# Chunk loop of a hybrid mLSTM decoder kernel: value weighting moved from GpSimd to ScalarE, mask addition moved from GpSimd to VectorE

## The reference

```python
a = g[..., None] - b + logi
m_new = jnp.maximum(g_j + m, a_j.max(-1))
w = jnp.exp(a_j - m_new[..., None])
C_new = decay[..., None, None] * C + jnp.einsum('bhl,bhld,bhle->bhde', w, k_j, v_j)
n_new = decay[..., None] * n + jnp.einsum('bhl,bhld->bhd', w, k_j)
...
log_d = jnp.where(causal, b[..., :, None] - b[..., None, :] + logi[..., None, :], -jnp.inf)
m_row = jnp.maximum(log_inter, log_d.max(-1))
p = jnp.einsum('bhcld,bhcsd->bhcls', q_c, k_c) * jnp.exp(log_d - m_row[..., None])
num = jnp.einsum('bhcls,bhcsd->bhcld', p, v_c) + w_inter[..., None] * jnp.einsum('bhcld,bhcde->bhcle', q_c, C_prev)
```

## Time and profile before

| | |
|---|---|
| median of 3 runs | 963.71 us (960.85 to 966.08) |
| the profiled execution, its own time | 963.89 us |
| its span, first to last instruction | 961.9 us |
| mean granted TensorE clock | 0.968 |
| TensorE products busy | 902.2 us (94%) |
| VectorE busy | 634.5 us (66%) |
| ScalarE busy | 454.6 us (47%) |
| GpSimd busy | 229.6 us (24%) |

### The profile page before, as it was taken

The page is one execution under the profiler, slowest core; times in us unless marked ns, Lnnn a source line. Parts: engine busy times, 40 slices in busy tenths (PEclk is TensorE's granted clock), DMA queues, the critical chain, the costliest instruction groups (busy, mean ns, idle before and its releaser), DMA issues.

```text
span 961.9 us, 15372 instructions
## 1 busy us (share of the span) xinstructions
PE 902.2 (94%) x5093; PEld 784.6 (82%) x5093; DVE 634.5 (66%) x945; ACT 454.6 (47%) x609; POOL 229.6 (24%) x239
## 2 busy tenths in 40 slices
PE   8999999999998899999889999999999999999930
PEld 8998887888776788888678988988988988988930
DVE  3432599895339877777874389385789974335727
ACT  4532101010258434422516489485789966345626
POOL 3100010001121121000022453453445442424410
PEclk9999999999999899999999999999999999999975
DMA  8620213111754444445486789888799997738256
GB/s 294 215 95 3 99 44 131 56 45 44 252 167 141 156 152 170 170 154 197 139 325 178 238 298 386 277 303 330 241 365 391 383 381 261 227 76 295 45 128 265
DMA packets 72963, 195.18 MB, mean 203 GB/s; under 512 B 9582, under 2 KB 23488, under 8 KB 72928
## 3 DMA queue, kind: packets, MB, share of 16 engines
q1 hardware_dynamic: 60976, 156.43, 44.5%
q0 software_dynamic: 11808, 38.15, 14.6%
q10 hardware_dynamic: 144, 0.14, 0.1%
HBM read 158.95 MB, written 35.74 MB: 202 GB/s over the span
## 4 chain that ended last, share of the span: by engine, by line
PE 89%; DVE 6%; issue 2%; DMA 1%; ACT 1%; POOL 0%; SPq 0%; DVEq 0%; POOLq 0%; ACTq 0%
PE banks L655 14%; PE banks L1155 14%; PE banks L644 14%; PE banks L669 14%; PE banks L1152 9%; PE banks L1295 9%; PE banks L1219 4%; PE banks L628 2%; PE banks L1327 1%; PE banks L635 1%; PE banks L1270 1%; PE banks L1273 1%; DVE arena L929 1%; PE banks L1315 1%; DVE arena L1788 1%
## 5 line engine op out<-in xcount | busy, mean ns | idle before, releaser
L697 DVE TENSOR_TENSOR split_weights<-arena,split_weights 128x1024 fp32r<-128x1024 f32 x192 | 223.2, 1221 | 0.0
L693 ACT ACTIVATE split_weights<-arena 128x1024 fp32r<-128x1024 f32 x192 | 190.8, 1054 | 3.9 <-DMA arena<-in_w_down 2.1
L655 PE MATMUL banks<-split_weights,split_rows 128*128 128x256 f32 x1152 | 147.5, 284 | 0.0
L655 PEld LDWEIGHTS banks<-split_weights,split_rows 128*128 128x128 f32 x1152 | 142.7, 191 | 1.9
L1155 PE MATMUL banks<-split_weights 128*128 128x512 f32 (+2 forms) x768 | 136.4, 338 | 1.7 <-DVE split_weights L1592 1.6
L669 PE MATMUL banks<-split_weights,split_hidden 128*128 128x512 f32 x576 | 137.5, 394 | 0.0
L644 PE MATMUL banks<-split_weights,split_rows 128*128 128x512 f32 x576 | 136.2, 392 | 0.7 <-DVE split_rows L863 0.7
L1155 PEld LDWEIGHTS banks<-split_weights 128*128 128x128 f32 x768 | 118.7, 189 | 17.5 <-DVE split_weights L1586 2.1
L644 PEld LDWEIGHTS banks<-split_weights,split_rows 128*128 128x128 f32 x576 | 109.2, 190 | 23.6 <-issue 0.8
L669 PEld LDWEIGHTS banks<-split_weights,split_hidden 128*128 128x128 f32 x576 | 106.5, 188 | 21.6
L567 POOL DMA_INDIRECT sum_scratch<-work,tile_sums x24 | 95.3, 3971 | 113.3 <-ACT work L741 98.0
(11 more groups left out here) (322 smaller groups left out, 1079.7 us busy)
## 6 DMA issues: line engine op xcount, KB each, us to landing
arena<-in_w_gate SPq DMA_DIRECT2D x64, 512.0 KB
arena<-in_w_up SPq DMA_DIRECT2D x64, 512.0 KB
arena<-in_w_down SPq DMA_DIRECT2D x64, 512.0 KB
arena<-in_w_in SPq DMA_DIRECT2D x20, 512.0 KB
arena<-in_x SPq DMA_DIRECT2D x16, 512.0 KB, 6.2
arena<-in_w_out SPq DMA_DIRECT2D x8, 512.0 KB
x_scratch<-arena SPq DMA_DIRECT2D x8, 512.0 KB, 3.5
sum_scratch<-arena SPq DMA_DIRECT2D x8, 512.0 KB, 4.7
```

Of the source, the lines that this page charges most:

```text
L655: last = pe.matmul(bank(up_bank[a])[:, 0:DH2], XR[:, hx, k, :], wu[:, hw, k, a * DH2:(a + 1) * DH2], start=(k == 0 and i == 0), stop=(k == ...
L693: act.activation(unit_split(u, 0), unit_slot(u), AF.Copy).then_inc(xw_hi, 1)
L697: dve.tensor_tensor(unit_split(u, 1), unit_slot(u), unit_split(u, 0).bitcast(F32), ALU.subtract).then_inc(xw_lo, 1)
```

## The change

GpSimd's `step` in the chunk loop is taken out, and with it its eleven elementwise instructions there. ScalarE gets `weigh_v` as four ACTIVATE instructions (copy with a scale, one for each head) at the end of its step, behind `split_h`. VectorE gets `mask` as one TENSOR_TENSOR between `update_state` and the first half's residual. The waits of both move with them; VectorE also waits once, ahead of the loop, for the columns of ones. GpSimd still weights chunks 0 and 1 and masks chunks 0 to 2 ahead of the loop.

```diff
-            def step(ch):
-                if 1 <= ch.n < T - 1:
-                    weigh_v(ch.plus(1))
-                if 1 <= ch.n < T - 2:
-                    mask(ch.plus(2))
-
-            chunk_steps(pool, step)
             pool_experts(pool, own)
...
+            def weigh_v(ch):
+
+                b = ch.b
+                act.wait_ge(v_in[b], 16 * ch.r + 16)
+                act.wait_ge(state_ps, ch.c)
+                for h in range(HEADS):
+                    last = act.activation(vw[:, h, :], vau[b][:, h, :], AF.Copy, scale=w4[:, 0, bass.ds(ch.c * HEADS + h, 1)])
+                last.then_inc(vw_sb, 1)
+
...
                 if n < T:
                     split_h(ch)
+                if n < T - 1:
+                    weigh_v(ch.plus(1))
...
+            def mask(ch):
+
+                v = nm[ch.b]
+                dve.wait_ge(nm_in[ch.b], 16 * ch.r + 16)
+                dve.tensor_tensor(v, v, nmask.unsqueeze(1).to_broadcast([P, HEADS, P]), ALU.add).then_inc(nm_masked, 1)
+
+            dve.wait_ge(ones_col, 2)
...
                 if mixes:
                     update_state(ch)
+                if 1 <= n < T - 2:
+                    mask(ch.plus(2))
                 if projects:
                     residual1(ch.plus(-1), 0)
                     half_statistics1(ch.plus(-1), 0)
```

## The result

The changed kernel takes **958.82 us** in the median of 5 runs (956.70 to 959.86), the kernel before 963.69 us (960.85 to 966.08). The ratio is 0.9947 with a 95% interval of 0.9929 to 0.9965: 4.9 us less. The forecast was 959.0 us.

The account below looks back on a forecast made before the run. The prediction took TensorE to bound the kernel, except in step 1, where TensorE waits for VectorE, which GpSimd stops. 963.89 - 2.52 (line 1788) - 2.40 (clock) = 958.97, say 959.0 us, with a range of 955.5 to 963.0 us.

Parts of the forecast that it names:

- What bounds the kernel: The chain is TensorE for 89% and VectorE for 6%; only in step 1 does something other than TensorE decide.
- Line 1788's term: In step 1, VectorE's four instructions of line 1788 go from 3.65 to 1.13 us: 2.52 us less.
- The clock's term: In step 1, TensorE's lines 1337 and 1295 take 3.37 in place of 5.77 us as the clock stays up: 2.40 us.
- The number of long steps: Of the five steps behind step 1, three take 20.84 and not 19.20 us; count kept, 1.64 us each.
- The moved pieces at nothing: ScalarE's four ACTIVATEs, 1.28 us, and VectorE's mask, 0.69 us, lie in idle time of the steps: cost 0.
- the slack: Idle time left: ScalarE 0.25 us, with 1.70 us behind it; VectorE 1.25 us in the loop, 1 us in step 1.
- part of a rival: Another wait of step 1, such as the row split behind late ln1 rows, takes the 2.5 us: near 963, chance 0.10.
- The clock did not fall: Rival: step 1's gap shrinks but the clock falls all the same, losing the 2.40 us: 961.4 us, chance 0.22.
- the slower rival: VectorE's wait for the maxima ahead of the mask delays TensorE in each of five steps: 969 us, chance 0.04.

Follow-up runs that it names:

- the two instructions whose results nobody uses: The changed kernel with two unused TENSOR_TENSORs on GpSimd, reading SBUF, where step 1's two pieces stood: 962.79 us.
- the memsets: The changed kernel with four unused memsets of 128x512 on GpSimd in step 1's place, writing SBUF and reading nothing: 958.91 us.
- The filler in the kernel before: The kernel before, with 12 products that nobody reads in TensorE's gap ahead of step 1's head transposes: 962.27 us.

## Why the prediction was right, and where it was loose

**What bounds the kernel.** Step 1 was named as the one place where something other than TensorE decides. The two kernels that move step 1 alone, and all but step 1, bear that out: 958.95 and 963.76 us.

**Line 1788's term, 2.52 us.** Measured 3.65 - 1.14 = 2.51 us, and TensorE's wait went from 3.70 to 1.19 us where 1.18 was forecast. The cause, GpSimd reading SBUF, is shown by the two instructions whose results nobody uses, and by the memsets, which don't read and left line 1803 at 0.69 us. One reading was loose: GpSimd was not silent beside the 1.13 us of the earlier trace rows, since its line 1078 started at 357.37 under the last of the four. There it was GpSimd that took longer, 1.25 us in place of 1.07. The 1.13 us are right all the same: in step 1 of the changed kernel and in all behind it the four take 1.13 or 1.14 us.

**The clock's term, 2.40 us.** The chain has 0.63 + 2.77 = 3.40 us where 5.77 stood, 2.37 us. Step 1 fell by 5.10 us, the two terms measure 4.88; the rest is the two transposes of line 1339 behind them, 0.43 us at the low clock and 0.22 us now, which the sum had left out. The numerators, 1.78 us in both, were at full speed already. The filler in the kernel before shows that it was the clock: 2.56 us of the step came back with VectorE as slow as ever. In the median of runs that filler gave back only 1.4 us, with an interval that holds 2.4 as well as nothing, so the size of this term rests on profiles.

**The number of long steps, left at three.** It was two in the changed kernel's profile, and two or three of five in all the others without products in the steps. The runs of one kernel spread by 3.2 us (changed) and 5.2 us (before), those of the kernels without long steps by 1.5 to 2.5 us. Each run also lists its mean granted clock. In the 63 runs of the kernel before that stand beside the experiments a higher clock goes with a shorter time: the median is 964.65 us for the 35 runs at 0.968, 962.75 us for the 13 at 0.971 and 960.58 us for the 5 at 0.973. So much of the spread is the clock, and that it is the number of long steps is likely but not shown, since only one run of each kernel has a profile. The profiled run of the changed kernel had the highest clock of its five, 0.975 against 0.970 to 0.973, so its two long steps need not be what the median run had.

**The moved pieces at nothing.** Right: 1.27 and 0.68 us, forecast 1.28 and 0.69, neither with a wait of TensorE behind it. What was loose is the slack. The prediction reads it in step 4, a long step, and estimates 1 us for step 1, where the row split ended at 322.99 and the projection's next products started at 324.34. The tightest is step 2, with 0.15 us left behind the wait for the LayerNorm rows, which the prediction had only as part of a rival.

**The rivals.** The clock did not fall at a gap of 1.19 us, in any of the eight profiles that have it. It did once at 2.48 and once didn't at 2.69 us. The wait for the maxima, the slower rival, never appeared: the mask has no idle time before it in the profile.

**The sum.** 959.0 forecast, 958.82 measured. That it fits to 0.2 us is luck beyond the two terms, since a single long step is worth 1.64 us and the two kernels' runs spread by 3.2 and 5.2.

## What to carry to other kernels

Look at what a lightly loaded engine does to its neighbours before moving its work: here 24% busy GpSimd held no chain, yet two of its instructions cost 5 us, because VectorE stood still for them at the one place where TensorE waited for VectorE. Here TensorE's wait of 3.7 us had two prices, the 2.51 us that could be saved of it and 2.37 us of low clock behind it. Where a gap or a run of narrow products cannot be removed, a few products that nobody reads can be worth more than they cost: two in each of five steps gave 958.82 to 954.60 us. And before adding work to an engine's idle time, read the slack in the tightest step and not in a typical one.

## What was not expected of the hardware

A VectorE instruction that meets two GpSimd instructions in a row waits for both: a single one of 0.35 us took 2.87 us. The loss was 1.29 or 1.50 us with one GpSimd instruction and 2.51 us with two, so the 0.2 us beyond GpSimd's own time come once and not for each.

The waiting goes both ways. In step 3 of the kernel before, GpSimd's two instructions started while VectorE was inside one with two operands in SBUF, and they took longer:

```profile
357.37 1.25 POOL L1078 TENSOR_TENSOR work<-work,small 128x516 f32<-128x516 f32 x1 [18.45 <-PE banks L1281]
...
358.58 1.74 POOL L1070 TENSOR_TENSOR arena<-arena,work 128x512 f32<-128x512 f32 x1
```

In step 1 they took 1.07 and 1.27 us. And the granted clock fell in steps whose TensorE work is the same as that of steps where it stayed: two products in a wait of 0.48 us, in a step of 19 us, decided about 1.65 us.
